# A hybrid decoder layer on one core: sampled tokens packed into one stationary for v and r, low-rank gates stacked by depth, banks handed back by thirds

## What is computed

```python
hn = rms_norm(x, norm_mix)
proj = hn @ w_in                      # GLU a,b | q | k | v (1024) | r (1024) | a_low (16) | gates
u_glu, q, k, v, r, a_low, gate_c, gate_g = jnp.split(proj, split_points, axis=-1)
conv_out, new_buf = conformer_conv(u_glu, ...)          # depthwise, width 31, then LayerNorm, silu
log_a = log_sigmoid(a_low @ w_gla_gate_up + b) / 16     # (16 x 512), the "low-rank" gates
o, new_s = gla_recurrence(q * DK**-0.5, k, v, log_a, gla_s, chunk)
gla_out = (rms_norm(o, gla_norm_g) * silu(r)) @ w_gla_out
h = x + (sigmoid(gate_c) * conv_out + sigmoid(gate_g) * gla_out) @ w_out
h = h + hier_moe(rms_norm(h, norm_ffn), ...)            # 32 experts, top 2; final RMSNorm after
```

## Time and profile before

| | us |
|---|---|
| median of 3 runs | 1757.73 (1754.54 to 1759.61) |
| the profiled execution, its own time | 1755.28 |
| its span | 1753.6 |
| PE busy | 1671.7 (95%) |
| DVE busy | 1249.8 (71%) |
| ACT busy | 920.2 (52%) |
| POOL busy | 222.5 (13%) |

### The profile page before, as it was taken

The page is one execution under the profiler, slowest core; times in us unless marked ns, Lnnn a source line. Parts: engine busy times, 40 slices in busy tenths (PEclk is TensorE's granted clock), DMA queues, the critical chain, the costliest instruction groups (busy, mean ns, idle before and its releaser), DMA issues.

```text
span 1753.6 us, 24797 instructions
## 1 busy us (share of the span) xinstructions
PE 1671.7 (95%) x8928; PEld 1471.5 (84%) x8928; DVE 1249.8 (71%) x2079; ACT 920.2 (52%) x1172; POOL 222.5 (13%) x260
## 2 busy tenths in 40 slices
PE   7999999999999999999999987999999999999991
PEld 6999987777999999879998876888888888888771
DVE  5234799986676667655464558998989898888873
ACT  6263121216433344325333336788888787777864
POOL 3100111000000000001001222311111111211110
PEclk9999999999999999999999998999999999999996
DMA  5401223222243222355343338999999999999965
GB/s 196 142 26 73 73 97 105 92 80 79 76 141 119 90 90 91 100 194 195 126 167 124 109 128 361 338 366 370 368 387 385 386 390 391 378 375 387 358 214 204
DMA packets 103439, 366.99 MB, mean 209 GB/s; under 512 B 14461, under 2 KB 57681, under 8 KB 89536
## 3 DMA queue, kind: packets, MB, share of 16 engines
q1 hardware_dynamic: 80448, 308.76, 47.3%
q0 software_dynamic: 22704, 57.12, 10.1%
q10 hardware_dynamic: 208, 0.08, 0.0%
HBM read 325.13 MB, written 61.22 MB: 220 GB/s over the span
## 4 chain that ended last, share of the span: by engine, by line
PE 67%; PEld 19%; DMA 5%; DVE 4%; issue 2%; ACT 1%; PEldq 1%; DVEq 0%; ACTq 0%; SPq 0%; POOLq 0%
PE bank L1005 64%; PEld bank L1005 19%; PE bank L1436 1%; DMA wraw_up<-in_w_expert_up 1%; DMA wraw_down<-in_w_expert_down 1%; PE bank L1460 1%; DVE fbuf L2586 1%; DVE wL_down L1965 1%; DVE wL_up L1965 1%; PE bank L1357 0%; DMA cw_raw<-in_w_conv_out 0%; DVE wL_gate L1965 0%; PE bank L1014 0%; DMA wo_in<-in_w_out 0%; DMA uo<-in_x_prompt 0%
## 5 line engine op out<-in xcount | busy, mean ns | idle before, releaser
L1965 DVE TENSOR_TENSOR wL_down<-wraw_down,wH_down 128x1024 fp32r<-128x1024 f32 x144 | 166.7, 1220 | 32.2 <-ACT wH_down L1534 31.9
L1965 DVE TENSOR_TENSOR wL_up<-wraw_up,wH_up 128x2048 fp32r<-128x2048 f32 x72 | 161.6, 2286 | 20.3 <-ACT wH_up L1534 20.3
L1965 DVE TENSOR_TENSOR wL_gate<-wraw_gate,wH_gate 128x2048 fp32r<-128x2048 f32 x72 | 161.8, 2288 | 13.8 <-ACT wH_gate L1534 13.5
L1534 ACT ACTIVATE wH_up<-wraw_up 128x2048 fp32r<-128x2048 f32 x72 | 134.0, 1910 | 63.7 <-DMA wraw_up<-in_w_expert_up 39.8
L2079 DVE SCALAR_TENSOR_TENSOR ybuf<-uo,gwork,ybuf 128x1024 f32<-128x1024 f32 x120 | 153.7, 1281 | 6.1 <-issue 6.1
L1534 ACT ACTIVATE wH_down<-wraw_down 128x1024 fp32r<-128x1024 f32 x144 | 140.4, 1053 | 11.6 <-DMA wraw_down<-in_w_expert_down 11.6
L1534 ACT ACTIVATE stage<-bank 128x512 f32<-128x512 f32 (+4 forms) x63 | 33.4, 545 | 198.3 <-PE bank L1005 191.0
L1534 ACT ACTIVATE wH_gate<-wraw_gate 128x2048 fp32r<-128x2048 f32 x72 | 134.5, 1934 | 1.7 <-DMA wraw_gate<-in_w_expert_gate 1.7
L1005 PE MATMUL bank<-nTH,gateH 128*128 128x352 f32 x384 | 132.1, 344 | 0.6 <-issue 0.6
L1005 PE MATMUL bank<-nTH,slabH 128*128 128x352 f32 x384 | 125.9, 328 | 2.4 <-DVE nTL L1965 1.8
L949 POOL DMA_INDIRECT h_scr<-ybuf,kdT x36 | 71.3, 1981 | 433.1 <-ACT ybuf L1534 397.6
(11 more groups left out here) (316 smaller groups left out, 4248.3 us busy)
## 6 DMA issues: line engine op xcount, KB each, us to landing
wraw_gate<-in_w_expert_gate SPq DMA_DIRECT2D x36, 2048.0 KB, 15.1
wraw_up<-in_w_expert_up SPq DMA_DIRECT2D x36, 2048.0 KB
wraw_down<-in_w_expert_down SPq DMA_DIRECT2D x36, 2048.0 KB
slab_raw<-in_w_in SPq DMA_DIRECT2D x7, 2048.0 KB, 8.4
gate_scr<-stage POOLq DMA_DIRECT2D x16, 528.0 KB, 3.5
vr_scr<-stage POOLq DMA_DIRECT2D x32, 256.0 KB, 2.3
gate_raw<-in_w_in SPq DMA_DIRECT2D x16, 512.0 KB, 9.3
vrbuf<-vr_scr SPq DMA_DIRECT2D x16, 512.0 KB, 7.3
```

Of the source, the lines that this page charges most:

```text
L1534: return act.activation(out, in_, func, **kw)
L1965: return dve.tensor_tensor(out, x, y, op)
```

## The change

1. Job tile 8 of v and r. ACT copies the sampled tokens' high and low parts side by side into `n_samples` (128 x 8 x 64). `packed` makes two matmuls per k: the 64 columns against the high slab, the 32 high columns against the low slab. The bank's rows 0 to 31 and 32 to 63 are summed later: ACT evicts both, POOL adds them before its spill (m = 8, 17, 26); for m = 35 DVE evicts and adds, after `level_diffs` of chunk 0. ACT no longer evicts job 35. The sampled r is stored without silu, which ACT now applies after the load.
2. `a_low` comes out three times (96 columns, in strides of 32), the second copy is turned into the low part by DVE, `wup_stack` holds high, high, low: a Z job is one float32r matmul of depth 96 per bank.
3. `taken` counts thirds: 3 per job, and PE waits for the third it is about to overwrite.
4. `LN_JOB` is 28, 30, 32. ACT's `last_factors(0, 0)` moves from ahead of the wait for all spills to between the second and third `gate_out` of chunk 0. `slab_low(2, ...)` on DVE starts one Z job earlier. PE's levels wait for two jobs less than all of `staged`, and for all of it ahead of the output products.

```diff
-        LN_JOB = (27, 29, 31)
+        LN_JOB = (28, 30, 32)
 (POOL, start)
-            pool.wait_ge(const_step, 6)
-            pool.dma_start(wup, a["w_gla_gate_up"][0]).then_inc(early_loaded, 16)
+            pool.memset(wup, 0.0).then_inc(const_step, 1)
+            pool.wait_ge(const_step, 7)
+            for part in range(3):
+                pool.dma_start(flat(ybuf)[part * S_T:part * S_T + RANK, D:D + QK], a["w_gla_gate_up"][0]) \
+                    .then_inc(early_loaded, 16)
 (POOL, spills of v and r)
+                if t == NCH and m < VRJ - 1:
+                    pool.tensor_tensor(src, src, st3[3][0:S_T, :], ALU.add)
+                    pool.drain()
 (PE)
+            def packed(out, xhl, xh, wh, wl, first, stop):
+                mm(out[0:2 * S_T, :], xhl, wh, first, False, skip_group_check=True)
+                return mm(out[0:S_T, :], xh, wl, False, stop, skip_group_check=True)
...
                 for j in range(3):
+                    if 2 <= n < N_K + 2:
+                        pe.wait_ge(taken[n % 2], 3 * (n // 2) - 2 + j)
                     last = unit(bk[3 * (n % 2) + j], j)
...
-                    project(n, lambda out, j: mm(out[0:P, 0:BLK], wup[:, h * DK:(h + 1) * DK], alow[:, third(j)],
-                                                 True, True))
+                    project(n, lambda out, j: mm(out[0:P, 0:BLK], wup_stack[:, h * DK:(h + 1) * DK],
+                                                 alow[:, third(j)], True, True))
...
+                    else:
+                        last = packed(bk[m % 6], n_samples[:, k, :], n_samples[:, k, 0:S_T], slabH[s % 2][:, k, :],
+                                      slabL[s % 2][:, k, :], k == 0, k == KC - 1)
 (ACT)
-                    last.then_inc(taken[n % 2], 1)
+                        if p != 2:
+                            last.then_inc(taken[n % 2], 1)
...
+            f(n_samples[:, :, 0:S_T], nTH[:, :, SEQ:T], ACT.Copy)
+            f(n_samples[:, :, S_T:], nTL[:, :, SEQ:T], ACT.Copy)
...
-            last_factors(0, 0)
...
+                    if j == 2 and isinstance(c, int) and c == 0:
+                        last_factors(0, 0)
                     gate_out(c, 0, j)
...
+            act.wait_ge(rc_loaded, 16 * (NCH + 1))
+            f(rch[0:R, :], rch[0:R, :], ACT.Silu)
 (DVE)
+            dve.wait_ge(abs_ln_made, 1)
+            tt(wup_stack[2 * S_T:AK, :], wup[2 * S_T:AK, :], wup_stack[2 * S_T:AK, :].bitcast(F32), ALU.subtract)
+            for j in range(3):
+                last = tt(alow[S_T:2 * S_T, third(j)], bk[j][S_T:2 * S_T, 0:BLK], alow[S_T:2 * S_T, third(j)].bitcast(F32),
+                          ALU.subtract)
+            last.then_inc(taken[0], 3)
...
             level_diffs(0, 48)
+            dve.wait_ge(vr_ready, m + 1)
+            dve.tensor_copy(st3[m % 3][0:S_T, :], bk[m % 6][0:S_T, :])
+            dve.drain()
+            tt(st3[m % 3][0:S_T, :], bk[m % 6][S_T:2 * S_T, :], st3[m % 3][0:S_T, :], ALU.add).then_inc(staged, 1)
             level_products(0, 0)
```

More of the change, by code:

```diff
@@ L866, in _ @@
                 pool.wait_ge(staged, 2 * NU + m + 1)
-                src = st3[m % 3] if t < NCH else st3[m % 3][P - S_T:P, :]
+                src = st3[m % 3][0:rows(t), :]
+                if t == NCH and m < VRJ - 1:
+                    pool.tensor_tensor(src, src, st3[3][0:S_T, :], ALU.add)
+                    pool.drain()
                 pool.dma_start(vr_scr[col // 2, t * P:t * P + rows(t), (col % 2) * 512:(col % 2) * 512 + 512], src) \
@@ L1054, in project @@
                     pe.wait_ge(staged, NU + 3 * (n - 1 - N_K))
[L1055 to L1057 removed]
+                elif n < 2:
                     pe.wait_ge(staged, NU)
                 for j in range(3):
+                    if 2 <= n < N_K + 2:
+                        pe.wait_ge(taken[n % 2], 3 * (n // 2) - 2 + j)
                     last = unit(bk[3 * (n % 2) + j], j)
@@ L1063, in _ @@
             pe.wait_ge(low_made, 5)
-            project(0, lambda out, j: by_token(out[:, 0:BLK], lambda k: walH[:, k, :], lambda k: walL[:, k, :], third(j)))
-            pe.wait_ge(early_loaded, 16 * 5)
+            project(0, lambda out, j: by_token(out[0:AK, 0:BLK], lambda k: walH[:, k, 0:AK], lambda k: walL[:, k, 0:AK],
+                                               third(j)))
+            pe.wait_ge(early_loaded, 16 * 7)
             for n in range(1, 1 + H + CC):
@@ L1113, in _ @@
                 s = 4 + col
-                t0 = slice(t * P, (t + 1) * P) if t < NCH else slice(T - P, T)
+                t0 = slice(t * P, (t + 1) * P)
                 if t == 0:
@@ L1605, in _ @@
             for j in range(3):
-                last = f(alow[:, j * BLK:(j + 1) * BLK], bk[j][0:RANK, 0:BLK], ACT.Copy)
-            last.then_inc(taken[0], 1)
+                last = f(alow[:, j * BLK:(j + 1) * BLK], bk[j][0:AK, 0:BLK], ACT.Copy)
+            last.then_inc(abs_ln_made, 1)
             for n in range(1, 1 + H + CC):
@@ L1611, in _ @@
                 if n in B_JOB:
-                    for dst, src in u_parts(B_JOB.index(n), n):
+                    for p, (dst, src) in enumerate(u_parts(B_JOB.index(n), n)):
                         if n == B_JOB[0]:
@@ L1661, in _ @@
                 col, t = divmod(m, NT)
-                rs_ = slice(0, P) if t < NCH else slice(P - S_T, P)
+                if m == VRJ - 1:
+                    continue
                 act.wait_ge(vr_ready, m + 1)
                 act.wait_ge(spilled[m % 3], 16 * ((2 * NU + m) // 3))
-                f(st3[m % 3][rs_, :], bk[m % 6][rs_, :], ACT.Copy if m < VRJ // 2 else ACT.Silu) \
-                    .then_inc(staged, 1)
+                if t < NCH:
+                    f(st3[m % 3], bk[m % 6], ACT.Copy if m < VRJ // 2 else ACT.Silu).then_inc(staged, 1)
+                else:
+                    act.wait_ge(state_out, 16 * sum(x < m for x in NEWC_JOB))
+                    if col:
+                        act.wait_ge(spilled[(m - NT) % 3], vr_spilled(m - NT))
+                    f(st3[m % 3][0:S_T, :], bk[m % 6][0:S_T, :], ACT.Copy)
+                    f(st3[3][0:S_T, :], bk[m % 6][S_T:2 * S_T, :], ACT.Copy).then_inc(staged, 1)
                 if t in (1, 2, 3, 4) and col < 3:
@@ L2041, in _ @@
                 last.then_inc(b_made, 1)
-                if h >= 2:
-                    slab_low(2, h - 2)
-            for part in range(2, 4):
-                slab_low(2, part)
+                if h >= 1:
+                    slab_low(2, h - 1)
+            slab_low(2, 3)
             for c in range(CC):
@@ L2049, in _ @@
                 dve.wait_ge(proj_ready, n + 1)
-                dve.wait_ge(taken[n % 2], n // 2)
+                dve.wait_ge(taken[n % 2], 3 * (n // 2))
                 for dst, src in u_parts(c, n):
                     last = tt(dst, src, dst, ALU.mult)
-                last.then_inc(taken[n % 2], 1)
+                last.then_inc(taken[n % 2], 3)
                 dve.drain().then_inc(u_made, 1)
```

59 lines of the change are left out of this document (40 added, 19 removed).

## The result

| | kernel before | changed kernel |
|---|---|---|
| median of the first measurement | 1757.6 us (6 runs) | 1745.1 us (1740.9 to 1748.3, 6 runs) |
| ratio | | 0.9927, 95% interval 0.9915 to 0.9938 |
| measured again, in another group of runs | 1757.8 us (17 runs) | 1746.7 us (6 runs), 0.9940 (0.9921 to 0.9958) |
| profiled execution, its span | 1755.3, 1753.6 us | 1748.3, 1746.6 us |

By the two ratios the change makes the kernel 10.5 to 12.8 us faster; 11.2 were forecast, and a median of 1746.5. The runs disagree by as much as 2 us on the size, so they can't confirm the sum to a tenth. Two of its terms were wrong, and what follows is mainly about them.

What follows compares the result with a forecast made beforehand. Bound: PE, busy 95%, nearly waitless from 84 to 470 us; expert stage also near the DMA limit. 7.5 + 5.3 + 0.3 - 1.5 - 0.4 = 11.2 us less, median 1746.5, range 1741.5 to 1753.

Steps and rivals of the forecast that it cites:

- v and r, 7.5 us: Tile 8 in column three: 32 fewer PE matmuls at 0.233 us each save 7.5 us.
- Z jobs and slab, 5.6 us: Four Z jobs save 1.33 us each, 5.3 (2.1 if thirds did nothing); the vanished slab wait saves 0.3.
- LayerNorm one job later, "by itself worth nothing": Before the LayerNorm: DVE's convolution slack 7.4 us with job 28, 1.8 with old jobs; no wait either way, worth nothing.
- POOL's three adds lie in its idle time: Sampled v and r: POOL's three adds fall where POOL is idle; no cost was counted for them.
- The end of r, minus 1.5: PE waits 1.0 us at the third gate block and 0.4 for `kdT`; cost 1.5 with restarts, bounds 0 to 8.9.
- Sampled silu, minus 0.4: ACT's later silu of sampled r delays its next eviction 1.0 us; PE waits 0.4, bounds 0 to 1.
- POOL's start, "I put them at nothing; if that cover were gone at most 2": At the start, POOL's added memset and two DMAs run ahead of the first transposes: nothing, at most 2 us.
- no wait above 3 us in chunk 0: Rival at r's end: late spill or stage buffer stalls PE 5 to 9 us; price 6, 1752.5 us, chance 0.07.
- no fall of the clock in narrow jobs: Rival in packed and Z jobs: narrow matmuls lower PE's clock, 24 us at half pace, 1770.5 us; chance 0.04.
- thirds that do help: Rival at the Z jobs: thirds do not help, gain 2.1 us instead of 5.3, 1750 us; chance 0.05.
- Given back in the expert stage: Rival: expert weight loads, not PE, set the end, so the earlier start is lost; 1757 us, chance 0.06.
- The prediction's own sign: Expert stage: the forecast would be wrong if it became longer by more than 3 us.

Runs made afterwards that it cites:

- e2: Kernel before with packed v and r jobs, job 35 on DVE, later silu, moved factors and later LayerNorm, without the Z-job part: 1751.8 us, 0.9971.
- e11: Changed kernel with 128 columns as stationary of both matmuls in the packed jobs, instead of 64 and 32: 1747.1 us, 0.9943 to before.
- e1: Kernel before with only the stacked Z jobs, three copies of `a_low`, the thirds and the earlier `slab_low(2, ...)`: 1750.1 us, 0.9959.
- e4: Changed kernel with the LayerNorm jobs back at 27, 29, 31: 1750.1 us, 0.9958 to before.
- e7: Changed kernel with LayerNorm jobs back at 27, 29, 31 and POOL's three adds removed: 1746.2 us, 0.9941 to before.
- e3: Changed kernel with PE waiting for whole bank sets instead of thirds: 1748.6 us, 0.9951 to before.
- e5: Changed kernel itself, unedited, measured and traced a second time: 1746.7 us, 0.9940 to before.
- e10: Changed kernel with job 35 handled like jobs 8, 17 and 26, evicted by ACT and added by POOL: 1751.3 us, 0.9963 to before.

## Why the prediction was right, and where not

*v and r, 7.5 us:* right, 7.52 in e2. The 0.233 us held for stationaries of 64 and 32 columns, as the earlier trace rows had it, and in e11 width changed nothing beyond 0.04 us. The Trainium skill's 131 ns (TensorE: Matmul & The Clock Gate, "Back-to-back issue gap") would have given 4.2; the runs do not agree with it and stay with the row.

*Z jobs and slab, 5.6 us:* right, 5.91 in e1; a job gave 1.39 instead of 1.33. Thirds 3.1, where the two cases (5.3 and 2.1) differ by 3.2.

*LayerNorm one job later, "by itself worth nothing":* wrong. It is worth 2.3 us at the gate block (e4). At the first level e4 loses 3.3, of which 0.9 are ACT's order. The step that failed is "POOL's three adds lie in its idle time": POOL was idle, but its adds take turns with DVE's convolution, the one chain that had no gap. They cost DVE 3.1 us (its slack was 4.32 where 7.4 were forecast). The later LayerNorm gave DVE the 5.6 us in which these vanish, so the sum came out right although this step was wrong: that is luck. With only these jobs put back (e4), the forecast would have been 3.3 us off. The Trainium skill states the mechanism (SBUF — State Buffer, "Who interferes with whom"): a DVE instruction with two inputs in SBUF contends with a GpSimd instruction that reads SBUF, and the port pair that they share is an exclusive lock. The convolution's operations read `uo` and `ybuf`, two such inputs; the 1.28 us at 379.21 and e7 agree.

*The end of r, minus 1.5:* right in kind, 1.06 measured (13.50 at the gate, 12.44 at the level). The third gate block came 0.2 us late and not 1.0, since the spill landed 2.0 us after its issue and ACT's two copies were short; the wait for `kdT` was 0.5 for 0.4.

*Sampled silu, minus 0.4:* half of it at most. PE waits 0.2 us for ACT's `mix_raw` in six of the ten traces that have this edit, and not in the other four, nor in the three without it.

*POOL's start, "I put them at nothing; if that cover were gone at most 2":* wrong, 0.8 us. The step looked at POOL's instructions and who waits for them. It did not ask what the two added loads share with others: the prompt's third tile came 0.5 to 1.0 us late with them (most likely through the DMA engines, which are full then), and the first q unit of PE with it.

*The sum:* 13.5 up to the gate, 1.1 given back there, 0.1 for the silu, 0.8 at the start: 11.5 us, where the forecast was 11.2, and the medians give 12.5 and 11.1. The terms ahead of the start were 1.1 too small in sum and the start's 0.8 was missing, so part of this closeness is chance. The first pair of profiled executions shows only 7.0 less span: 2.9 of the rest are the slow stretch in the first expert, and in the start the changed one had 19 matmuls at half pace to 11, another 1.1.

*Rivals:* no wait above 3 us in chunk 0, no fall of the clock in narrow jobs (1.00 from 84 to 470 us), thirds that do help (e3). "Given back in the expert stage" fails at its price of 10 us: the steady blocks start 11.6 us earlier in e5, and in the first trace they go at nearly the rate of the earlier trace rows, with the DMA engines at 0.99 again:

```profile
1114.70:1522.90 408.20, 407.68 (x1927) 341.56 (x1926) 361.78 (x272) 326.48 (x316) 64.52 (x46) 1.00 0.99 379
```

A part of it may hold all the same. The prediction's own sign, an expert stage longer by more than 3 us, is met by the first trace (659.9 us against 654.9, of which 2.9 are the slow first expert), and e5's is 2.6 longer. From the first steady block to the end, the thirteen traces take 628.1 to 632.6 us, and those that come to it earlier tend to take longer (632.6 from 1111.87, 631.9 from 1114.71, 630.2 from 1123.42, 628.1 from 1124.87; a line through all has 0.2 us more for each us earlier). That would give back about 2 us of 11.6, and e5's span is in fact only 9.1 us under before's. Of the 2.4 us by which e5's end part is longer than before's, 1.3 lie ahead of the last down product and 1.3 in that product (24 matmuls in 8.64 us instead of 7.36, the clock falls in both, for longer in e5). One trace of each kernel doesn't settle it, and no run tests it.

## What to carry to other kernels

An idle engine is not a free one: before work is put on it, look at what it shares with the engine that has no gaps (here POOL with DVE), and at what its DMAs share with the loads that PE waits for. An edit that looks worthless by the slack of before may pay for another edit; take it out alone before calling it nothing, and check that nothing else moved with it (here ACT's factors). And a hand-over in thirds is worth its whole price only once the work that hid the hand-over has become short: nothing before the stack, 3.1 us after it.

## What the runs showed of the hardware

- POOL's add of 32 x 512 took 1.3 us or 2.2 to 2.5 beside DVE's convolution, and 4.59 beside its level products (e10). One DVE operation beside each add of the convolution's time was about 1.04 us longer: 1.28 instead of 0.24, or 2.32 instead of 1.28 for the one on 1024 elements (the first add in e4 and e5).
- At the start PE works at half pace for 9 to 19 matmuls of the first q unit, and the views print a granted clock of 1.00 all the same. In all thirteen traces the record of the clock begins only where the pace changes (at 25.6 us in the changed kernel, 22.5 in before); ahead of it the 1.00 stands for no record, and the distance between starts (0.29 or 0.16 us) tells the clock.
- Three small loads of 32 KB in place of one, on POOL's queue, put a 512 KB tile on SP's queue off by up to 1 us.
- The matmuls of 512 columns started 0.23 us apart with a stationary of 128, 64 or 32 columns (e11 and the changed kernel).
